# Hybrid attention layer on eight cores: order of work from several scheduler passes, gate rows through DRAM, loads behind folded weights, and a last tile finished in halves

## What is computed

```python
mod = silu(c) @ w_ada + b_ada              # shift, scale, gate for both sub-layers
h = rmsnorm(x, norm_mix_g) * (1 + scale1) + shift1
z = h @ w_in                               # 1440 columns: latents, rotary key, window q, k, v
mix = concat(mla_group(z), swa_group(z))   # 8 dense causal heads, 8 heads on a 128 window
x = x + gate1 * (mix @ w_o)
h = rmsnorm(x, norm_mlp_g) * (1 + scale2) + shift2
x = x + gate2 * (square(relu(h @ w_up)) @ w_down)
out = rmsnorm(x, final_g)
```

## Time and profile before

| | |
|---|---|
| median of 3 runs | 765.85 us (764.91 to 768.96) |
| profiled execution | 765.9 us |
| its longest span (core 1) | 764.4 us |
| spans of the eight cores | 758.2 to 764.4 us |
| PE, DVE, ACT, POOL busy on core 1 | 93%, 73%, 59%, 30% of the span |

### The profile page before, as it was taken

The page is one execution under the profiler, slowest core; times in us unless marked ns, Lnnn a source line. Parts: engine busy times, 40 slices in busy tenths (PEclk is TensorE's granted clock), DMA queues, the critical chain, the costliest instruction groups (busy, mean ns, idle before and its releaser), DMA issues.

```text
span 764.4 us, 17786 instructions; the slowest of 8 cores (758.2 to 764.4 us)
## 1 busy us (share of the span) xinstructions
PE 713.9 (93%) x5970; PEld 447.4 (59%) x5970; DVE 555.5 (73%) x982; ACT 450.1 (59%) x753; POOL 232.9 (30%) x210
## 2 busy tenths in 40 slices
PE   0679999999899999999999989999999999999996
PEld 0344556556556555554666647766667766676652
...
GB/s 193 235 211 192 226 177 55 135 153 141 129 44 117 219 139 195 262 264 270 263 180 175 233 232 119 208 96 158 239 171 103 215 223 181 202 16 192 52 61 220
DMA packets 77801, 131.81 MB, mean 172 GB/s; under 512 B 40592, under 2 KB 48400, under 8 KB 75536
## 3 DMA queue, kind: packets, MB, share of 16 engines
...
HBM read 119.71 MB, written 29.10 MB: 195 GB/s over the span
## 4 chain that ended last, share of the span: by engine, by line
PE 87%; DMA 7%; issue 2%; DVE 2%; POOL 1%; ACT 1%; DVEq 0%; ACTq 0%; POOLq 0%
PE ps L998 27%; PE ps L1702 23%; PE ps L1927 22%; PE ps L1408 7%; PE ps L1432 4%; DMA arena<-wada 4%; DMA arena<-wup 4%; PE ps L1454 2%; PE ps L1478 1%; PE ps L1096 1%; PE ps L1293 1%; DVE arena L1084 0%; DVE arena L1136 0%; ACT arena L1458 0%; DVE arena L1161 0%
## 5 line engine op out<-in xcount | busy, mean ns | idle before, releaser
L998 PE MATMUL ps<-arena 128*128 128x512 bf16 (+2 forms) x1484 | 248.2, 300 | 20.8 <-DMA arena<-wada 16.4
L1702 PE MATMUL ps<-arena 128*128 128x256 bf16 x1680 | 199.6, 273 | 3.4 <-DMA arena<-wup 2.9
L1927 PE MATMUL ps<-arena 128*128 128x512 bf16 x840 | 197.1, 381 | 0.0
L1702 PEld LDWEIGHTS ps<-arena 128*128 128x128 bf16 x1680 | 163.4, 98 | 41.8 <-issue 9.7
L998 PEld LDWEIGHTS ps<-arena 128*128 128x128 bf16 x1484 | 105.5, 98 | 105.9 <-issue 29.5
L1416 ACT ACTIVATE arena<-ps 128x1024 bf16<-128x1024 f32 (+1 forms) x160 | 138.1, 896 | 47.2 <-PE ps L1408 21.4
L1890 DVE TENSOR_TENSOR arena<-ps,arena 128x512 f32<-128x512 f32 x194 | 128.1, 685 | 18.9 <-PE ps L1927 14.5
L1615 POOL TENSOR_TENSOR arena<-arena 128x512 bf16<-128x512 f32 x64 | 81.6, 1288 | 194.3 <-DVE arena L1827 75.1
L1927 PEld LDWEIGHTS ps<-arena 128*128 128x128 bf16 x840 | 82.6, 98 | 83.6 <-issue 2.9
L1688 DVE TENSOR_TENSOR arena<-ps,arena 128x512 f32<-128x512 f32 x90 | 61.7, 689 | 49.7 <-PE ps L1702 35.6
L1827 DVE TENSOR_TENSOR arena<-arena 128x1024 bf16<-128x1024 bf16 (+1 forms) x108 | 94.4, 887 | 4.2 <-DMA arena<-wup 2.9
...
## 6 DMA issues: line engine op xcount, KB each, us to landing
arena<-hss SPq DMA_DIRECT2D x12, 1792.0 KB, 7.8
arena<-x SPq DMA_DIRECT2D x32, 512.0 KB, 8.7
arena<-wdn SPq DMA_DIRECT2D x64, 256.0 KB, 5.8
arena<-wada POOLq DMA_DIRECT2D x24, 512.0 KB, 11.2
arena<-wup POOLq DMA_DIRECT2D x16, 512.0 KB, 13.5
out<-arena SPq DMA_DIRECT2D x15, 512.0 KB, 2.7
hss<-arena SPq DMA_DIRECT2D x4, 1792.0 KB, 7.8
x1s<-arena SPq DMA_DIRECT2D x12, 512.0 KB, 6.5
```

What stands on the lines that cost most here:

```text
L998: S.op("pe", lambda h, i=i: h.matmul(out, lhsT=lhs_list[i], rhs=rhs_list[i], start=(i == 0), stop=(i == n - 1)), r=rbufs[i], w=[bankb[bank]])
L1702: S.op("pe", lambda h, k=k, c0=c0, fc=fc, wv=wv, hv=hv, b=b, first=first: h.matmul(bk(b, None, (fc * 256, fc * 256 + 256)), lhsT=wv[:, k, ...
L1927: S.op("pe", lambda h, f=f, av=av, wv=wv, p=p, b=b, first=first, n=n, key=key: h.matmul(bk(b), lhsT=av[:, f, p * 128:(p + 1) * 128], rhs=w ...
```

## The change

1. `plan()` takes the place of the single `schedule()`. After each of ten passes, `latest()` works out backward from the modelled end how late each operation may start, and `mixed()` mixes the rank by that time with the first priority, in a share that differs from pass to pass (`MIX_`). The pass with the shortest modelled end is made again as the eleventh and written out.
2. `load_gate` makes one matmul of 8 x 128 and one ACT copy; one DMA writes the row to DRAM and a second loads it, broadcast to 128 partitions. Both are on SP.
3. `load_mix` of G = 0 waits for the folded `w_o` piece of its quad, that of G = 1 for piece 4.
4. `REFILL_OFF` is 200 instead of 400.
5. Tiles 14 and 15 are finished in halves. The first half's sum goes in as the bias of the logarithm, the gain product goes to a buffer of its own, the mean is taken by the scale of the square, and tile 15's scaling is in three pieces.

```diff
-REFILL_OFF = 400
+REFILL_OFF = 200
+LAST_OFF = 40
+HALVES = 14
+ROUNDS = 10
+MIX_ = (0.5, 0.25, 0.75, 0.05, 0.9)
...
+        deps = [list(o.deps) for o in self.all]
+        pri = first = [o.pri for o in self.all]
+        best = None
+        for k in range(ROUNDS + 1):
+            if k == ROUNDS:
+                pri = best[1]
+            for o, d, p in zip(self.all, deps, pri):
+                o.deps, o.pri, o.taken = list(d), p, False
+                for t in o.tens:
+                    t.i, t.left = None, len(t.ops)
+            try:
+                self.schedule()
+            except RuntimeError:
+                self.makespan = None
+            if self.makespan is not None and (best is None or self.makespan < best[0]):
+                best = (self.makespan, pri)
+                late = self.latest()
+            pri = self.mixed(first, late, k)
+
+    def latest(self):
+        after = [[] for _ in self.all]
+        for o in self.all:
+            for (d, dv, kind) in o.deps:
+                after[d.idx].append(o)
+        nxt = {}
+        for e in self.ENGS:
+            for a, b in zip(self.ops[e], self.ops[e][1:]):
+                nxt[a.idx] = b
+        late = [0.0] * len(self.all)
+        for o in sorted(self.all, key=lambda o: -o.start):
+            t = self.makespan
+            for x in after[o.idx]:
+                t = min(t, late[x.idx] - (0.0 if x.eng == o.eng and not o.dma else self.LAT[x.eng] if not o.dma else 0.0))
+            t -= (o.npk * o.pk + 2100.0) if o.dma else o.dur + (165.0 if o.eng == "pe" else 0.0)
+            if o.idx in nxt:
+                t = min(t, late[nxt[o.idx].idx] - o.dur)
+            late[o.idx] = t
+        return late
+
+    def mixed(self, first, late, k):
+        n = sorted(range(len(late)), key=lambda i: late[i])
+        rank = [0] * len(late)
+        for r, i in enumerate(n):
+            rank[i] = r
+        a = MIX_[k % len(MIX_)]
+        return [a * r + (1 - a) * p for r, p in zip(rank, first)]
...
         def load_gate(i):
             dst, bdst = ((G1B, bG1), (G2B, bG2))[i]
             c0 = (16, 40)[i]
-            for half in range(2):
-                b = take_bank(RB)
-                for c in range(4):
-                    j = c0 + half * 4 + c
-                    S.op("pe", lambda h, j=j, c=c, b=b: h.matmul(
-                        bk(b, None, (c * 128, c * 128 + 128)), lhsT=MODCOL[:, j:j + 1].to_broadcast([128, 128]), rhs=IDENTF,
-                        start=(c == 0), stop=(c == 3)), r=[bMOD[j // 2], bIDFB], w=[bankb[b]])
-                S.op("act", lambda h, half=half, b=b: h.activation(out=dst[:, half * 512:(half + 1) * 512], in_=bk(b), func=AF.Copy),
-                     r=[bankb[b]], w=[bdst])
+            b = take_bank(RB)
+            S.op("pe", lambda h: h.matmul(bk(b, (0, 8), (0, 128)), lhsT=MODCOL[:, c0:c0 + 8], rhs=IDENTF, start=True, stop=True),
+                 r=bMOD[c0 // 2:c0 // 2 + 4] + [bIDFB], w=[bankb[b]])
+            S.op("act", lambda h: h.activation(out=GROW, in_=bk(b, (0, 8), (0, 128)), func=AF.Copy), r=[bankb[b]], w=[bGROW])
+            S.dma("sp", lambda h: h.dma_start(out=gate_d[i].rearrange("(a b) -> a b", a=8, b=128), in_=GROW), bGD[i], r=[bGROW], w=[bGD[i]])
+            S.dma("sp", lambda h: h.dma_start(out=dst, in_=bcast_row(gate_d[i:i + 1, :], D)), bdst, r=[bGD[i]], w=[bdst])
...
         def load_mix(G, quad):
             mt = mt_slot[G, quad] = slots["mt"].take()
             S.dma("sp", lambda h: h.dma_start_transpose(out=MIXT[mt], in_=mx_d[G, quad]), bMIXT[mt],
-                  r=[bMXD[G][quad]], w=[bMIXT[mt]])
+                  r=[bMXD[G][quad]] + ([bWO[quad]] if G == 0 else [bWO[4]] if G == 1 else []), w=[bMIXT[mt]])
...
-                        if t == 15:
+                        if t >= HALVES:
                             final_half(t, half)
-                    if t < 15:
+                    if t < HALVES:
...
+        def final_parts(t):
+            st = ctr["fst", t] = nxt_of("sta", 4)
+            gained = {}
+
+            def mean_sq(half):
+                hs = slice(half * 512, (half + 1) * 512)
+                S.op("act", lambda h: h.activation(out=JUNK[:, hs], in_=X1[t][:, hs], func=AF.Square, scale=float(D) ** -0.5,
+                                                   accum_out=STA[st][:, half:half + 1]), r=[bX1[t][half]], w=[bSTA[st][half], bJUNK])
+
+            def gain(half):
+                hs = slice(half * 512, (half + 1) * 512)
+                v, bv = gained[half] = (WST[half], bWST[half]) if t == 15 else (RT[half], bRT[half])
+                S.op("dve", lambda h: h.tensor_tensor(out=v, in0=X1[t][:, hs], in1=FGB[:, hs], op=ALU.mult),
+                     r=[bX1[t][half], bFG], w=[bv])
+
+            def root():
+                S.op("act", lambda h: h.activation(out=STA[st][:, 3:4], in_=STA[st][:, 1:2], func=AF.Ln, bias=STA[st][:, 2:3]),
+                     r=[bSTA[st][1], bSTA[st][2]], w=[bSTA[st][3]])
+                S.op("act", lambda h: h.activation(out=STA[st][:, 4:5], in_=STA[st][:, 3:4], func=AF.Exp, scale=-0.5),
+                     r=[bSTA[st][3]], w=[bSTA[st][3]])
+
+            def eps_up():
+                S.op("act", lambda h: h.activation(out=STA[st][:, 2:3], in_=STA[st][:, 0:1], func=AF.Identity, bias=EPSC),
+                     r=[bSTA[st][0], bEPS], w=[bSTA[st][2]])
+
+            def scale_out(i, half, c0, c1, engs):
+                g, bg = gained[half]
+                v = g[:, c0:c1]
+                bo = Buf(f"o{t}_{i}")
+                fd = lambda h: h.tensor_scalar(out=v, in0=v, scalar1=STA[st][:, 4:5], scalar2=None, op0=ALU.mult)
+                fa = lambda h: h.activation(out=v, in_=v, func=AF.Copy, scale=STA[st][:, 4:5])
+                fs = {"dve": fd, "act": fa}
+                S.flex({e: fs[e] for e in engs}, r=[bg, bSTA[st][3]], w=[bo])
+                return bo
+
+            def store(half, bs):
+                g, bg = gained[half]
+                od = S.dma("sp", lambda h: h.dma_start(out=out_d[t * 128:(t + 1) * 128, 512 * half:512 * half + 512], in_=g),
+                           bFIN[(2 * t + half) % 4], r=bs + [bg])
+                S.final.append(od)
+
+            return mean_sq, gain, root, eps_up, scale_out, store
...
         def final_half(t, half):
-            hs = slice(half * 512, (half + 1) * 512)
             if half == 0:
-                ctr["fst"] = nxt_of("sta", 4)
-            st = ctr["fst"]
-            S.op("act", lambda h: h.activation(out=JUNK[:, 0:512], in_=X1[t][:, hs], func=AF.Square,
-                                               accum_out=STA[st][:, half:half + 1]), r=[bX1[t][half]], w=[bSTA[st][half], bJUNK])
-            S.op("dve", lambda h: h.tensor_tensor(out=X1[t][:, hs], in0=X1[t][:, hs], in1=FGB[:, hs], op=ALU.mult),
-                 r=[bX1[t][half], bFG], w=[bX1[t][half]])
+                ctr["fp", t] = final_parts(t)
+            mean_sq, gain, root, eps_up, scale_out, store = ctr["fp", t]
+            if t == 15:
+                S.prio(-LAST_OFF)
+            mean_sq(half)
             if half == 0:
-                return
-            S.op("dve", lambda h: h.tensor_tensor(out=STA[st][:, 2:3], in0=STA[st][:, 0:1], in1=STA[st][:, 1:2], op=ALU.add),
-                 r=[bSTA[st][0], bSTA[st][1]], w=[bSTA[st][2]])
-            rstd4(st, 2, 1, D)
-            bo = [Buf(f"o{t}_{i}", bX1[t][0].alloc) for i in range(2)]
-            S.op("dve", lambda h: h.tensor_scalar(out=X1[t][:, 0:512], in0=X1[t][:, 0:512], scalar1=STA[st][:, 10:11],
-                                                  scalar2=None, op0=ALU.mult), r=[bX1[t][0], bSTA[st][2]], w=[bo[0]])
-            S.op("act", lambda h: h.activation(out=X1[t][:, 512:1024], in_=X1[t][:, 512:1024], func=AF.Copy,
-                                               scale=STA[st][:, 10:11]), r=[bX1[t][1], bSTA[st][2]], w=[bo[1]])
-            for i in range(2):
-                od = S.dma("sp", lambda h, i=i: h.dma_start(out=out_d[t * 128:(t + 1) * 128, i * 512:(i + 1) * 512],
-                                                            in_=X1[t][:, i * 512:(i + 1) * 512]), bFIN[(2 * t + i) % 4],
-                           r=[bo[i]])
-                S.final.append(od)
+                eps_up()
+            gain(half)
+            if half == 1:
+                root()
+                if t == 15:
+                    store(0, [scale_out(0, 0, 0, 512, ("dve",))])
+                    store(1, [scale_out(1, 1, 128, 512, ("act",)), scale_out(2, 1, 0, 128, ("dve",))])
+                else:
+                    for i in range(2):
+                        store(i, [scale_out(i, i, 0, 512, ("act", "dve"))])
+            S.prio(0)
...
-        S.schedule()
+        S.plan()
```

8 lines of the change are left out of this document (6 added, 2 removed).

## The result

The changed kernel takes 755.0 us at the median of its four runs (754.4 without the highest, 816.1), the kernel before 765.55 (764.91 to 768.96). The ratio is 0.9849 with a 95% interval of 0.9818 to 0.9880. On another chip it was 0.9822 (0.9801 to 0.9844). Some executions of every kernel are disturbed and far longer; the ratios, and the times given for the experiments, leave them out. The forecast was 755.7 us, range 751.0 to 762.5.

The account below looks back on a forecast made before the run. TensorE on the slowest core was taken as the bound. Savings of 5.0 us per core and removed stalls gave core 1 750.3; with new chance delay the slowest was put at 754.2, plus 1.5 outside the span: 755.7 us, range 751 to 762.5.

Parts of the forecast that it names:

- The sum by cores: Span forecast per core: savings of 5.0 us on every core, plus each core's own stalls; core 1 from 764.4 to 750.3.
- the stalls that I had named: PE idle: core 1, 2.77 us at 191.53 and 2.94 at 457.38; core 3, 3.05 at 196.44; core 5, 2.10 at 380.35.
- small waits, for which I had allowed 1 us: About 1 us taken off core 1's sum without new delay to set the range's lower end at 751.
- Gate rows: One matmul per gate instead of eight saves 3.3 us on PE; two DMA landings of about 11 us cost nothing.
- Refill: REFILL_OFF of 200 issues the q=1 w_up loads near 411 us, 17 us earlier; core 1 gains 4.6 us.
- the w_up wait: PE idle for an up-projection weight, 2.94 us at 457.38 on core 1, also on the other seven; expected to go.
- The rival of late loads: The q=1 w_up loads land late all the same: 1 to 2 us wait plus 1.7 slow clock, 759.4 us; chance 0.06.
- Transposes: Mixed-head loads of G=0 moved behind the w_o folds, done near 229 us; priced at nothing, bounds 0 to 3 us.
- the stall at 191 us: Unexplained PE "issue" wait of 2.77 us at 191.53 on core 1, plus 1.7 for half clock; counted as gone.
- The end: Tail after PE's last row: half sums join in Ln's bias, scaling in three pieces; 1.7 us less (1.2 to 1.9).
- Core 5's kind of stall: PE idle 2.10 us at 380.35 behind DVE, which waited for an h2s store; if it decides, 757.7 us; chance 0.15.

## Why the prediction was right

**The sum by cores** was close: core 1 750.3 forecast and 750.2 measured, core 3 751 to 752.7 and 750.6, core 5 752.4 (its stall gone) and 752.6. That cores 1 and 5 fit to 0.2 us is luck: over four runs of the changed kernel core 1 takes 750.2 to 752.8 us, core 3 748.2 to 752.7, core 5 749.2 to 752.6. The other cores gained 2 us more than their terms in places (core 7: 753 and 750.7), from small waits, for which I had allowed 1 us. On the mean core PE's idle time fell by 4.8 us: 2.8 are the stalls that I had named, 2.0 smaller waits that had no term.

**Gate rows.** The 3.3 us are consistent with the old gates put back (5.1 us with the waits that came along). The landings were over-sized: I took 11 us for the two and they took 4.8 to 7.4. Traffic there is light (the DMA share from 186.7 to 191.5 us on core 5 is 0.28, in the kernel before on core 1 1.25). The row was 3.6 to 6.2 us early, 5 forecast, but that fits because two errors cancel: the fold came early as well, at 197.7 instead of near 203.

**Refill.** The mechanism is shown: with the one number changed the w_up wait goes, with it changed back the wait comes. The loads were issued at 407.65, 411 forecast. The margin was over-sized: on core 5 it is 4 us at the first sum and 1.3 at the second, where I had 3 to 10. The landings, 415 to 438, are near the 419 to 436 forecast; it is the second sum that came early, at 434.4 instead of 439. Each of the four loads takes longer than the one ahead of it (6.9, 15.5, 24.0, 28.0 us), so the third is the one to watch. The rival of late loads, given 0.06, missed by 1.1 us on core 3.

**Transposes.** I priced their wait at nothing and gave the stall at 191 us even odds of coming back elsewhere. With the wait alone that stall was on none of eight cores, where it had been on two; in the changed kernel it came back at 171 to 174 us, smaller, on two of eight. Without the wait the whole kernel lost 6 to 7 us. I wrote that nothing shows what the stall waited for; the instruction packets do. Such rows of 1.2 to 4 us also came at 171 to 176 us in several kernels and once at 257, so it is not a matter of these transposes only.

**The end** was mis-sized, 1.3 us at most for 1.7: the last Square started late behind ACT's other work, and on some cores the last store took up to 0.5 us longer to land.

**What my sum left out** is the passes. I took the order as a given and read stalls out of it. One pass with the same edits has a stall of 3.7 to 4.1 us on all cores and more small waits, which together eat nearly all of the gain, while the passes without the edits give nothing that can be told from zero. The change is worth 12 to 14 us by the two ratios, and its parts alone 2.7 (REFILL_OFF), 1.9 (transposes) and 0.6 us (passes). Taken out of the changed kernel one at a time they cost, by the mean span, 9.8 (passes), 5.9 (REFILL_OFF), 5.0 (transposes), 4.8 (gates) and 1.2 us (end), together far more than the whole is worth: the parts need each other. Since each experiment let the scheduler order everything anew, it tells the price of a part with the order that goes with it. A run with the order held and one part changed was not made.

**Core 5's kind of stall** was a rival with 0.15. It did not decide the changed kernel's profile but is still in the order, as the run with the old end shows.
